# Attention score products of two heads issued as one group on the two halves of TensorE's rows

## What is computed

```python
# block 1, dsa: 4 index heads of 64, then 8 heads of 64
dots = einsum('bqhd,bsd->bqhs', q_idx, k_idx) * 64 ** -0.5
scores = einsum('bqh,bqhs->bqs', w_idx, relu(dots))      # top 64 keys of each query
logits = einsum('bqhd,bqkhd->bqhk', q, k_sel) * 64 ** -0.5 + bias
# block 1, moba: 8 heads of 64, one block of 256 keys, so plain causal attention
logits = einsum('bqhd,bqhjld->bqhjl', q, k_g) * 64 ** -0.5 + bias
# block 2: 8 heads, each with two halves c of 64
logits = einsum('bqhcd,bkhcd->bhcqk', q, k) * 64 ** -0.5 + bias
p = softmax(logits);  attn = p[:, :, 0] - lam * p[:, :, 1]
```

## Time and profile before

| | before |
|---|---|
| median of 3 runs | 1052.75 us (1052.53 to 1054.51) |
| span of the profiled execution, first to last instruction | 1050.7 us |
| PE busy | 1040.1 us, 99% of the span |
| DVE busy, ACT busy, POOL busy | 627.7 us, 545.4 us, 122.4 us |
| mean share of the DMA engines, by slices | 1 to 8 tenths |
| granted TensorE clock | 1.000 |

### The profile page before, as it was taken

The page is one execution under the profiler, slowest core; times in us unless marked ns, Lnnn a source line. Parts: engine busy times, 40 slices in busy tenths (PEclk is TensorE's granted clock), DMA queues, the critical chain, the costliest instruction groups (busy, mean ns, idle before and its releaser), DMA issues.

```text
span 1050.7 us, 13219 instructions
## 1 busy us (share of the span) xinstructions
PE 1040.1 (99%) x4854; PEld 851.8 (81%) x4854; DVE 627.7 (60%) x868; ACT 545.4 (52%) x745; POOL 122.4 (12%) x110
## 2 busy tenths in 40 slices
PE   8999999999999999999999999999999999999998
PEld 6788888887777888888888887778888888888886
DVE  5545444668865667554454667666489766545553
ACT  7344343665655636444434575756875545443441
POOL 0000000122310000000000041109923000000000
PEclk9999999999999999999999999999999999999999
DMA  7776775584333455556556366444455545555641
GB/s 244 246 244 224 227 223 170 176 300 160 121 120 121 154 167 188 188 184 200 170 189 199 121 245 200 136 146 123 129 190 200 173 159 192 197 183 180 197 160 41
DMA packets 113815, 188.83 MB, mean 180 GB/s; under 512 B 4577, under 2 KB 60010, under 8 KB 113642
## 3 DMA queue, kind: packets, MB, share of 16 engines
q1 hardware_dynamic: 113754, 188.23, 54.7%
q10 hardware_dynamic: 16, 0.00, 0.0%
HBM read 182.45 MB, written 5.77 MB: 179 GB/s over the span
## 4 chain that ended last, share of the span: by engine, by line
PE 93%; DVE 2%; ACT 2%; DMA 1%; POOL 1%; issue 1%; SPq 1%; DVEq 0%; ACTq 0%; POOLq 0%
PE bank L1635 22%; PE bank L1637 21%; PE bank L1636 21%; PE bank L1730 6%; PE bank L1729 6%; PE bank L1731 6%; PE bank L1674 2%; PE bank L1647 1%; PE bank L1984 1%; PE bank L1856 1%; DVE hid L1351 1%; ACT hi L712 1%; POOL rstd_q L633 1%; PE bank L1970 1%; DMA resid<-in_x 1%
## 5 line engine op out<-in xcount | busy, mean ns | idle before, releaser
L1635 PE MATMUL bank<-hi,xh 128*128 128x512 f32 (+1 forms) x944 | 379.1, 402 | 2.1 <-DVE xl L1157 0.8
L1637 PE MATMUL bank<-hi,xl 128*128 128x512 f32 (+1 forms) x944 | 368.2, 390 | 0.0
L1636 PE MATMUL bank<-lo,xh 128*128 128x512 f32 (+1 forms) x944 | 366.7, 388 | 0.0
L1118 DVE TENSOR_TENSOR lo<-raw,hi 128x2048 fp32r<-128x2048 f32 x112 | 256.0, 2287 | 174.3 <-ACT hi L712 174.3
L712 ACT ACTIVATE hi<-raw 128x2048 fp32r<-128x2048 f32 (+1 forms) x116 | 220.6, 1903 | 142.1 <-PE bank L1731 98.5
L1635 PEld LDWEIGHTS bank<-hi,xh 128*128 128x128 f32 x944 | 177.4, 188 | 40.2 <-DVE xl L1157 1.9
L1637 PEld LDWEIGHTS bank<-hi,xl 128*128 128x128 f32 x944 | 177.2, 188 | 38.1
L1636 PEld LDWEIGHTS bank<-lo,xh 128*128 128x128 f32 x944 | 177.7, 188 | 33.5
L1135 DVE TENSOR_TENSOR lo<-raw,hi 128x1024 fp32r<-128x1024 f32 (+1 forms) x108 | 132.5, 1235 | 60.6 <-ACT hi L721 60.1
L1729 PE MATMUL bank<-hi,hh 128*128 128x512 f32 x304 | 119.8, 394 | 1.1 <-DVE hl L1181 1.1
L1730 PE MATMUL bank<-lo,hh 128*128 128x512 f32 x304 | 119.7, 394 | 0.0
(11 more groups left out here) (231 smaller groups left out, 945.2 us busy)
## 6 DMA issues: line engine op xcount, KB each, us to landing
raw<-in_w_in SPq DMA_DIRECT2D x48, 1024.0 KB
raw<-in_ffn_w_gu SPq DMA_DIRECT2D x84, 512.0 KB
raw<-in_ffn_w_down SPq DMA_DIRECT2D x22, 1024.0 KB
raw<-in_w_up SPq DMA_DIRECT2D x16, 1024.0 KB
raw<-in_w_down SPq DMA_DIRECT2D x16, 1024.0 KB
raw<-in_w_out SPq DMA_DIRECT2D x8, 1024.0 KB
distance_table<-ftab SPq DMA_DIRECT2D x8, 576.0 KB
raw<-in_w_proj_attn SPq DMA_DIRECT2D x4, 1024.0 KB
```

Of the source, the lines that this page charges most:

```text
L1118: nc.vector.tensor_tensor(lo[s][:, :, 0:width], raw[s][:, :, 0:width], hi[s][:, :, 0:width].bitcast(F32), ALU.subtract).then_inc(lo_done, 1)
L1635: nc.tensor.matmul(o, sh, wh, start=first and j == 0, stop=False)
L1636: nc.tensor.matmul(o, sh, wl, start=False, stop=False)
L1637: ins = nc.tensor.matmul(o, sl, wh, start=False, stop=last and j == 3)
```

## The change

The two steps `k` and `k + 1` (`k` even) are issued together, at the slot of `k`, by a new function: first the two products of 256 keys, on partitions 0 to 63 into bank2 and on 64 to 127 into bank3, then the two of 128 keys in the same turn. Nothing is issued at the slot of `k + 1`. The pair waits until both banks have been read, so for step `k - 1`, where it waited for step `k - 2` before. DVE, ACT, POOL and SP are unchanged.

```diff
+            def pair_scores(qt, qb, kt, kb, done):
+
+                upper, lower = slice(0, HD), slice(HD, 2 * HD)
+                nc.tensor.matmul(S[0][:, 0:SEQ], qt[upper, qb, P:SEQ], kt[upper, kb, :], start=True, stop=True)
+                nc.tensor.matmul(S[1][:, 0:SEQ], qt[lower, qb, P:SEQ], kt[lower, kb, :], start=True, stop=True)
+                nc.tensor.matmul(S[0][:, SEQ:SPAN], qt[upper, qb, 0:P], kt[upper, kb, 0:P],
+                                 start=True, stop=True).then_inc(done, 1)
+                nc.tensor.matmul(S[1][:, SEQ:SPAN], qt[lower, qb, 0:P], kt[lower, kb, 0:P],
+                                 start=True, stop=True).then_inc(done, 1)
...
-                if M1_DOTS <= p < M1_DOTS + NIDX:
+                if M1_DOTS <= p < M1_DOTS + NIDX and (p - M1_DOTS) % 2 == 0:
...
-                    if h >= 2:
-                        pe.wait_ge(m_relu, h - 1)
...
+                    if h == 0:
+                        pe.wait_ge(res_done, 4)
+                    else:
+                        pe.wait_ge(m_relu, h)
+                    pair_scores(idxt, h // 2, idxt, 2, m_dot)
                 k = at(M1_STEP, p)
-                if k >= 0:
...
+                if k >= 0 and k % 2 == 0:
+
+                    if k == 0:
+                        pe.wait_ge(m_relu, NIDX)
+                        pe.wait_ge(m_trev, 6)
                     else:
-                        pe.wait_ge(m_l, k - 1)
...
+                        pe.wait_ge(m_l, k)
...
+                    pair_scores(qt, k % NH // 2, kt, k % NH // 2, m_s)
...
                 k = at(M2_STEP, p)
-                if k >= 0:
-                    h, half = k // 2, k % 2
-                    if k >= 2:
-                        pe.wait_ge(k_l, k - 1)
+                if k >= 0 and k % 2 == 0:
+                    h = k // 2
                     if k == 0:
                         pe.wait_ge(k_trev, 4)
                         pe.wait_ge(res_done, 12)
+                    else:
+                        pe.wait_ge(k_l, k)
...
+                    pair_scores(q_2, h, k_2, h, k_s)
```

More of the change, by code:

```diff
@@ L1829, in _ @@
                     ins.then_inc(m_tr, 1)
-                if M1_DOTS <= p < M1_DOTS + NIDX:
+                if M1_DOTS <= p < M1_DOTS + NIDX and (p - M1_DOTS) % 2 == 0:
                     h = p - M1_DOTS
                     pe.wait_ge(m_trev, 2)
-                    pe.wait_ge(res_done, 4)
-                    if h >= 2:
-                        pe.wait_ge(m_relu, h - 1)
[L1837 to L1841, removed]
+                    if h == 0:
[3 more added lines that the diff above has]
+                    pair_scores(idxt, h // 2, idxt, 2, m_dot)
                 k = at(M1_STEP, p)
-                if k >= 0:
-                    if k < 2:
-                        pe.wait_ge(m_relu, 3 + k)
-                    else:
-                        pe.wait_ge(m_l, k - 1)
-                    if k == 0:
-                        pe.wait_ge(m_trev, 6)
+                if k >= 0 and k % 2 == 0:
+                    if k == 0:
+                        pe.wait_ge(m_relu, NIDX)
+                        pe.wait_ge(m_trev, 6)
+                    else:
+                        pe.wait_ge(m_l, k)
                     if k == NH:
                         pe.wait_ge(m_trev, 10)
-                    h = k % NH
                     qt, kt = (q_m, k_m) if k < NH else (q_a, k_a)
[L1855 to L1859, removed]
+                    pair_scores(qt, k % NH // 2, kt, k % NH // 2, m_s)
                 k = at(M1_STEP, p - 3)
```

## The result

| | before | after |
|---|---|---|
| median | 1052.64 us (1052.31 to 1054.51, 4 runs) | 1035.9 us (1034.76 to 1036.73, 4 runs) |
| ratio, 95% interval | | 0.9837 (0.9823 to 0.9851) |
| span of the profiled execution | 1050.7 us | 1033.7 us |
| PE busy | 1040.1 us | 1021.1 us |

The change takes 17.0 us off the span. The sign was right, and so was what bounds the kernel and what a change of rows costs; the term for the overlap was too small.

What follows compares the result with a forecast made beforehand. PE's stream was taken to bound the kernel. The span was 1050.7 - 14.8 (18 pairs at 0.82) + 0.6 (grown wait) = 1036.5 us; with 2.05 us for the median, 1038.6 us, range 1037.0 to 1047.0.

Steps and rivals of the forecast that it cites:

- what bounds the kernel: Whole span: PE's stream, busy 99%, sets the end, and every microsecond taken from it moves the end.
- what a change of rows costs: Each score step: going from 128 rows to 64 and back costs 0.40 us of its 1.04; saved once a pair, 7.2 us.
- the term for the overlap: In each pair, products of the two halves run beside each other, saving at best 0.42 us a pair.
- A: All pairs: both savings, fewer row changes and best overlap, 0.82 us a pair; 1038.6 us, chance 0.45.
- Waits added by the pair: At each pair, PE waits for both banks to be read out; costed at nothing.
- The grown wait in slot 26: First layer, slot 26: PE's 0.7 us wait for DVE's scaling of k grows by 0.6 us.
- POOL's convolution, nothing lost: Convolution on POOL before the last gate product: slack shrinks from 4.2 to 3.4 us, so nothing is lost.
- B: In each pair, halves overlap, but a load never precedes the start of the product before it; 1042.3 us, chance 0.20.
- C: In each pair, halves run one after another and only changes of row number are saved; 1045.9 us, chance 0.14.
- D: Three times in every pair, going from one half to the other empties the array; 1056.4 us, chance 0.09.
- its half: In each pair, only the 0.11 us load is bare at each of three half changes; 1051.5 us, chance 0.06.
- E: At the pairs, DVE falls behind and waits on both banks eat part of the saving; 1046.6 us, chance 0.06.

Runs made afterwards that it cites:

- grouped order: The changed kernel with each pair's products reordered: upper half 256 and 128 keys, then lower half 256 and 128 keys; 1035.36 us.
- the second layer alone: The kernel before with the change in the second mixing layer only (8 pairs of 18), first layer left as it was; 1043.96 us, ratio 0.9921.

## Why the prediction was right and wrong

**What bounds the kernel**: right. PE's stream set the time, and what was taken from it came off the end, but for one wait.

**One step costs 1.04 us, of which 0.40 us for the change of rows**: right. 0.39 us measured with both steps on one half, 0.35 us with a transpose between. One reading in it was loose: the 0.28 us of idle load engine is not that of each step but the mean of 0.35 us behind a portion and 0.17 us behind transposes. The cost of a step hardly depends on it (1.01 and 1.05 us saved a pair in the two layers).

**The best bound of the overlap, 0.42 us a pair**: wrong, and this is the step that failed. Measured are 0.65 us. It was built on two rules that I put in myself. The first: "A part can start beside one of the other half, but not before the parts ahead of it have started". The changed kernel itself shows the lower half's first part at 628.43, 7 ns after the upper half's first and 0.31 us before the upper half's second (628.74), which stands ahead of it; the kernel in grouped order shows a part starting 13 ns after the first though three parts ahead of it had not started. The second: "eight loads of 0.11 us, one after another." The rows after show loads of the two halves 7 ns apart, two of them at a time. The rows before, in which every product uses the same rows of the array as its neighbour or all of them, could not show either rule for two halves. I wrote that the trace does not show two halves in a row, and yet gave a "best" that was no bound; the true one was the full 0.64 us, the second step for free. 18 x (0.65 - 0.42) = 4.1 us is more than the whole miss of the span, 2.8 us. The difference is the wait that grew by 1.1 instead of 0.6 us, the 0.5 us at the start, and 0.39 instead of 0.40 in 18 pairs.

**Products of different row groups**: TensorE: Matmul & The Clock Gate of the Trainium skill, The mechanism, says that products in different row groups run together some 4 ns apart. The trace after shows 7 ns, so the rule holds, with the larger figure. The prediction put down the sum by this rule as that of A, and this was misread: if the second half starts some ns after the first and streams beside it, the pair saves the whole 0.64 us and not 0.42, and 0.65 were measured. The same section says that products keep the program's order in start and end. That did not hold here: in grouped order the lower half's first product starts ahead of the upper half's second, and the measurement decides.

**Waits added by the pair**: right to cost them at nothing. DVE L1262 is not in PE's waits. The view of L1781 puts 0.4 us of idle load engine down to it once, but that is the 0.35 us that stands ahead of every pair behind a portion, so it cost nothing more; and the second layer alone gave its full 8 pairs.

**The grown wait in slot 26**: the mechanism was right, the size followed the wrong pair. With 1.04 instead of 0.82 a pair the same reckoning gives five pairs for PE against four for the data, 1.0 us; measured are 1.1. PE reached the place at 287.43 instead of 292.23, 4.8 us earlier, the data 3.7 us earlier. The chain in the kernel after is another one, though (critical chain in order of time):

```profile
272.70 1.13 DVE lo L1135
273.84 0.34 DVE l L1258
...
274.59 0.60 DVE ss_q L1343
...
279.40 2.55 POOL rstd_q L633
...
281.97 7.29 DVE hid L1351
```

It no longer comes from PE's transposes of slot 22 but from DVE's own queue (the earlier trace rows for before), so part of that stretch goes at DVE's pace now: in 226 to 332 us of the kernel after DVE is busy 81.58 of 106 us. Of the 0.1 us over 1.0 I can't say whether it is that. In either kernel the wait ends with one long instruction: L1351 takes 0.69 us in the median of its 16 executions before, and 7.29 us here, where it starts beside POOL's L650, which runs from 281.91 to 288.70. Moving that POOL instruction is the other way to shorten the wait, and was not tried.

**POOL's convolution, nothing lost**: right, but the slack shrank more than I reckoned. The convolution's last instruction in the kernel after, and the load of the last gate product that needs it (L2018, which was L2020):

```profile
740.84 0.73 POOL L672 TENSOR_TENSOR xc<-xc,rg 128x256 f32<-128x256 f32 x1
...
743.77 0.41 PEld L2018 LDWEIGHTS bank<-xc,wax 128*128 128x128 f32 x2
```

The one ends at 741.57 and the other begins at 743.77, so 2.2 us are left of 4.2, where I had 3.4.

**The rivals**: B, C, D and its half are out by the rows of one pair, and E by PE's waits. None of them, nor a sixth, allowed for more than A. The range's lower end was A with less waiting, when it should have held the case in which the two halves share nothing, 18 x 1.04 = 18.7 us less 1.0 for the wait, 1035.0 us.

## What to carry to other kernels

Two fp32 products with a contraction of 64, one on partitions 0 to 63 and one on 64 to 127, with results in two banks, cost TensorE the time of one, loads included. Put such products next to each other; the two orders tried cost the same, and it costs only when more than about three parts of one half wait ahead of the other. It also saves a change between 128 and 64 rows, which costs 0.35 to 0.40 us each time that a portion lies between. After a gain on the engine that sets the time, look at the waits it already had: each of them can grow by what was gained between its source and its place. Here a wait of 0.7 us had become one of 1.8 us, and one number takes it away.

## What the runs showed of the hardware

Loads and products on the two halves of the rows go side by side, 7 ns apart. Products of the other half pass up to about three waiting parts: 13 ns with three ahead in the grouped order, 0.76 us behind the first upper load where eight upper parts stood ahead, 2.07 us where sixteen did. Whether both halves could write one bank at the same time was not tried.
